# Hybrid decoder layer on eight cores: order of tiles, norm and branch results changed, and four tiles of x transposed by DMA

## The reference

```python
ya = pool_mixer(xa, pool_w, pool_scale) * silu(ga)
yb = u * (tril(w_s) @ layernorm(v) + b_s) * silu(gb)     # in chunks of 128 rows, 8 heads
yc = attention(q, k_mem, v_mem) * silu(gc)               # 4 heads over 256 memory rows
y = concat(rmsnorm(ya), rmsnorm(yb), rmsnorm(yc))
out = x + rmsnorm(y @ W_out) * norm_post
```

## Time and profile before

| what | value |
| --- | --- |
| median of three runs | 1258.14 us |
| the profiled execution | 1258.87 us |
| its span on the slowest core (core 3) | 1257.2 us |
| spans of all cores | 1251.3 to 1257.2 us |
| TensorE matmuls busy | 1220.3 us (97%) |
| VectorE, ScalarE, GpSimd busy | 488.0, 475.9, 216.0 us |

### The profile page before, as it was taken

How to read it: one execution, slowest core, us unless ns; L and a number is a source line. 1 busy time by engine, 2 the same in 40 slices (tenths; PEclk the granted TensorE clock), 3 DMA queues, 4 the chain that set the end, 5 groups by cost and what they waited for, 6 DMA issues and landing times.

```text
span 1257.2 us, 17843 instructions; the slowest of 8 cores (1251.3 to 1257.2 us)
## 1 busy us (share of the span) xinstructions
PE 1220.3 (97%) x6224; PEld 582.0 (46%) x6224; DVE 488.0 (39%) x782; ACT 475.9 (38%) x892; POOL 216.0 (17%) x205
## 2 busy tenths in 40 slices
PE   6889999999999999999999999999989999999997
PEld 3345544444444455555554444444434444444443
DVE  4167624332232233444443233333222454343434
ACT  4377733422222232222225555555632232223222
POOL 1000001221211011111121111111222222222222
PEclk9999999999999999999999999999999999999999
DMA  9945322554234452645435541441975492533231
GB/s 210 245 152 173 69 81 68 105 90 83 50 67 81 83 93 45 107 88 91 97 63 98 86 82 34 81 88 34 178 212 138 129 307 75 178 133 118 93 109 68
DMA packets 50938, 137.83 MB, mean 110 GB/s; under 512 B 22785, under 2 KB 35201, under 8 KB 37137
## 3 DMA queue, kind: packets, MB, share of 16 engines
q0 software_dynamic: 7632, 50.86, 24.3%
q1 hardware_dynamic: 43218, 85.83, 21.3%
HBM read 153.39 MB, written 29.36 MB: 145 GB/s over the span
## 4 chain that ended last, share of the span: by engine, by line
PE 90%; DMA 3%; DVE 2%; ACT 2%; issue 1%; SPq 0%; DVEq 0%; POOLq 0%; POOL 0%; ACTq 0%
PE ps L279 89%; DMA mem_pages<-x 2%; DMA mem_pages<-y_scr 2%; PE ps L282 1%; ACT mem_pages L391 1%; DVE mem_pages L395 1%; DVE mem_pages L1155 0%; ACT mem_pages L1030 0%; SPq L291 0%; ACT L1030 0%; DVE stat L1025 0%; DVE mem_pages L1127 0%; DVE mem_pages L1035 0%; DVE mem_pages L545 0%; ACT stat L256 0%
## 5 line engine op out<-in xcount | busy, mean ns | idle before, releaser
L279 PE MATMUL ps<-mem_pages 128*128 128x512 bf16 (+2 forms) x5760 | 1195.7, 369 | 7.9 <-DMA mem_pages<-y_scr 4.0
L279 PEld LDWEIGHTS ps<-mem_pages 128*128 128x128 bf16 x5760 | 555.7, 98 | 630.5 <-issue 22.8
L713 POOL TENSOR_TENSOR mem_pages<-mem_pages 128x512 f32<-128x512 f32 x72 | 91.1, 1266 | 599.9 <-ACT mem_pages L706 597.3
L700 ACT ACTIVATE mem_pages<-mem_pages,small_c 128x512 bf16<-128x512 f32 x96 | 68.8, 716 | 275.4 <-DVE mem_pages L772 148.1
L1127 DVE SCALAR_TENSOR_TENSOR mem_pages<-ps,stat,mem_pages 128x512 f32<-128x512 f32 x128 | 96.0, 750 | 166.8 <-PE ps L279 144.4
L1135 POOL TENSOR_TENSOR mem_pages<-mem_pages 128x512 f32<-128x512 f32 x64 | 81.1, 1267 | 257.3 <-ACT jk L1132 257.3
L1132 ACT ACTIVATE jk<-mem_pages 128x512 bf16<-128x512 f32 x64 | 40.3, 629 | 224.0 <-DVE mem_pages L1127 224.0
L903 DVE TENSOR_TENSOR mem_pages<-mem_pages 128x526 f32<-128x526 f32 (+3 forms) x80 | 56.1, 701 | 100.8 <-ACT mem_pages L897 95.8
L762 DVE TENSOR_TENSOR mem_pages<-ps,mem_pages 128x512 f32<-128x512 f32 x32 | 22.1, 691 | 141.3 <-PE ps L279 141.3
L732 ACT ACTIVATE mem_pages<-ps 128x512 f32<-128x512 f32 x96 | 54.5, 590 | 22.8 <-PE ps L279 19.4
L748 DVE CAST mem_pages<-ps 128x512 bf16<-128x512 f32 (+1 forms) x24 | 14.4, 601 | 124.6 <-PE ps L279 121.4
(11 more groups left out here) (66 smaller groups left out, 422.9 us busy)
## 6 DMA issues: line engine op xcount, KB each, us to landing
mem_pages<-w_pages POOLq DMA_DIRECT2D x44, 1024.0 KB, 12.9
mem_pages<-x SPq DMA_DIRECT2D x32, 1024.0 KB, 7.8
out<-mem_pages SPq DMA_DIRECT2D x15, 1024.0 KB, 4.7
y_scr<-mem_pages SPq DMA_DIRECT2D x96, 128.0 KB, 1.9
mem_pages<-y_scr SPq DMA_DIRECT2D x12, 1024.0 KB, 14.6
mem_pages<-w_pages POOLq DMA_DIRECT2D x8, 512.0 KB, 19.7
mem_pages<-mem SPq DMA_DIRECT2D x2, 1024.0 KB, 6.2
mem_pages<-mem_norm SPq DMA_DIRECT2D x1, 1024.0 KB
```

The costliest lines, as they stand in the source:

```text
L279: return lambda e: e.matmul(out, lhsT=lhsT, rhs=rhs, start=start, stop=stop)
L700: P.op("act", lambda e: e.activation(out=yv, in_=tmp, func=AF.Copy, scale=gbr[:, c:c + 1]), reads=[tmp_b[i], gbr_b], writes=[ring_b[r]])
L713: P.op("pool", lambda e: e.tensor_tensor(out=accl_v if last else acc, in0=acc, in1=dst, op=ALU.add), reads=[dst_b, acc_b[tb]], writes=[acc ...
```

## The change

It has five parts. In the front, the loads of tiles 4 and 5 of x wait for earlier weight tokens, the norm of tile 4 stands ahead of the LayerNorm halves, and the matmuls of tile 3 are spread between those of tiles 0 to 2. In the loop, tile 4's (1, 0) group comes ahead of tile 5's transposes, and a tile of x is loaded right behind the norm that frees its buffer. Tiles 9, 11, 13 and 15 are normed at the end of the turn three tiles earlier and transposed by one DMA each. In C, norm_post and y's first pages are loaded ahead of the third set of W_out pages. And the last tile's last 512 columns are worked in two halves of 256.

```diff
@@ -247,6 +247,7 @@
     ST_SSX, ST_RSX, ST_VS, ST_VQ, ST_VM, ST_VR, ST_VT = 0, 20, 40, 56, 72, 88, 104
     ST_RBR, ST_MX, ST_NB, ST_RI, ST_RS, ST_SO, ST_FO, ST_FR = 120, 168, 176, 184, 192, 256, 320, 336
     ST_LH0, ST_LH1 = 352, 360
+    ST_SL = 368
     ST_EPS = 383
 
     def sc(i):
@@ -546,7 +547,7 @@
                                               scalar2=sc(ST_VR + tt), op0=ALU.add, op1=ALU.mult),
              reads=[bank[b], bank[b + 1], s1], writes=[vn_b[tt]])
 
-    W2, W3, W4 = wbuf(("v", 0, 1)), wbuf(("v", 1, 0)), wbuf(("v", 1, 1))
+    W1, W3, W4 = wbuf(("v", 0, 0)), wbuf(("v", 1, 0)), wbuf(("v", 1, 1))
     x_a(0)
     x_a(1)
     x_a(2)
@@ -554,8 +555,8 @@
     x_pe(1, halves=(0,))
     x_a(3)
     x_pe(2, halves=(0,))
-    x_load(4, [W2[0].wtok])
-    x_load(5, [W4[0].wtok])
+    x_load(4, [W1[0].wtok])
+    x_load(5, [W3[1].wtok])
     x_load(6, [W4[1].wtok])
     x_load(7)
     x_pe(0, halves=(1,))
@@ -574,9 +575,9 @@
     for part in range(2):
         for tt in range(4):
             v_mm(tt, 0, 1, part)
-            if part == 1:
-                v_ln_half(tt, 0)
     x_a(4)
+    for tt in range(2):
+        v_ln_half(tt, 0)
     drop(*VN, dyn=False)
     take(*VN)
     vn_b += [nbuf("vn%d" % tt, VN[tt // 4]) for tt in range(NTT)]
@@ -584,19 +585,19 @@
         for tt in range(3):
             v_mm(tt, 1, 0, part)
     x_pe(4, (7, 7), (0,))
+    for tt in range(2, 4):
+        v_ln_half(tt, 0)
     v_mm(0, 1, 1, 0)
     v_mm(1, 1, 1, 0)
     x_pe(4, (7, 7), (1,))
     v_mm(2, 1, 1, 0)
-    v_mm(3, 1, 0, 0)
-    v_mm(3, 1, 0, 1)
     for tt in range(3):
+        v_mm(3, 1, tt // 2, tt % 2)
         v_mm(tt, 1, 1, 1)
         v_ln_half(tt, 1)
         v_ln_end(tt)
         if tt == 1:
             x_a(5)
-    v_mm(3, 1, 1, 0)
     v_mm(3, 1, 1, 1)
     v_ln_half(3, 1)
     v_ln_end(3)
@@ -630,20 +631,29 @@
                 out=tsg[:, h, :], in0=psb(b, q * 128, (q + 1) * 128), scalar=lnb[:, h:h + 1], in1=tsg[:, h, :],
                 op0=ALU.mult, op1=ALU.add), reads=[bank[b], tsg_b, small_b], writes=[tsg_b])
 
+    DT = (9, 11, 13, 15)
+    x_load(8)
+    x_load(9)
     for tt in range(4, NTT):
         v_mm(tt, 0, 0)
         v_mm(tt, 0, 1)
-        if tt + 1 < NTT:
+        if tt == 4:
+            v_mm(tt, 1, 0)
+        if tt + 1 < NTT and tt + 1 not in DT:
             x_pe(tt + 1)
-        if tt + 2 <= NTT:
+        if tt + 2 <= NTT and tt + 2 not in DT:
             x_a(tt + 2)
+            x_load(tt + 6)
         if tt + 2 == NTT:
             x_dma(NTT)
-        v_mm(tt, 1, 0)
+        if tt > 4:
+            v_mm(tt, 1, 0)
         v_mm(tt, 1, 1)
         v_ln(tt)
-        if tt + 4 <= NTT:
-            x_load(tt + 4)
+        if tt + 3 in DT:
+            x_a(tt + 3)
+            x_load(tt + 7)
+            x_dma(tt + 3)
         if tt + 4 > NTT:
             drop(xt_p[tt % NX])
             if tt == NTT - 1:
@@ -1099,7 +1109,7 @@
 
     def take_orow(tt):
         p = dyn()
-        orow[tt] = (p, [nbuf("or%d_%d" % (tt, db), p) for db in range(4)], nbuf("orr%d" % tt, p))
+        orow[tt] = (p, [nbuf("or%d_%d" % (tt, db), p) for db in range(5)], nbuf("orr%d" % tt, p))
 
     def load_xres(tt):
         p = dyn()
@@ -1107,55 +1117,56 @@
         dma_sp(page_f(p), x_d[tt * 128:(tt + 1) * 128, :], writes=[b], sem="d_ps%d" % p)
         xres[tt] = (p, b)
 
-    def wo_unit(tt, db):
+    def wo_unit(tt, db, lo=0, n=512, so=None):
         tb = tt // 4
+        so = ST_SO + tt * 4 + db if so is None else so
         p, obs, _ = orow[tt]
-        ov = page_f(p)[:, db * 512:(db + 1) * 512]
+        ob = obs[db + (1 if lo else 0)]
+        c0 = db * 512 + lo
+        ov = page_f(p)[:, c0:c0 + n]
         bks = []
         for br in range(3):
             b = balloc()
             yv = page_bf(ypage[(tb, br)][0]).rearrange("p (c t) -> p c t", c=8)
             Wo = w8(("wo", db, br))
-            fns = [mm(psb(b), yv[:, q, (tt % 4) * 128:(tt % 4 + 1) * 128], Wo[:, q, :], q == 0, q == 7)
+            fns = [mm(psb(b, 0, n), yv[:, q, (tt % 4) * 128:(tt % 4 + 1) * 128], Wo[:, q, lo:lo + n], q == 0, q == 7)
                    for q in range(8)]
             P.group("pe", fns, reads=[ypage[(tb, br)][1], wbuf(("wo", db, br))], writes=[bank[b]])
             bks.append(b)
         rc = ST_RBR + tt
-        P.op("act", lambda e: e.activation(out=ov, in_=psb(bks[0]), func=AF.Identity, scale=sc(rc)),
-             reads=[bank[bks[0]], rbr_b[tb]], writes=[obs[db]])
+        P.op("act", lambda e: e.activation(out=ov, in_=psb(bks[0], 0, n), func=AF.Identity, scale=sc(rc)),
+             reads=[bank[bks[0]], rbr_b[tb]], writes=[ob])
         for br in (1, 2):
             P.op("dve", lambda e, br=br: e.scalar_tensor_tensor(
-                out=ov, in0=psb(bks[br]), scalar=sc(rc + br * 16), in1=ov, op0=ALU.mult, op1=ALU.add),
-                reads=[bank[bks[br]], rbr_b[tb], obs[db]], writes=[obs[db]])
+                out=ov, in0=psb(bks[br], 0, n), scalar=sc(rc + br * 16), in1=ov, op0=ALU.mult, op1=ALU.add),
+                reads=[bank[bks[br]], rbr_b[tb], ob], writes=[ob])
         bfree(*bks)
-        so = ST_SO + tt * 4 + db
-        P.op("act", lambda e: e.activation(out=jk_v, in_=ov, func=AF.Square, scale=D ** -0.5, accum_out=sc(so)),
-             reads=[obs[db]], writes=[jk_b, so_b[tt]])
-        gv = page_f(gp["p"])[:, db * 512:(db + 1) * 512]
+        P.op("act", lambda e: e.activation(out=jk_v[:, 0:n], in_=ov, func=AF.Square, scale=D ** -0.5,
+                                           accum_out=sc(so)),
+             reads=[ob], writes=[jk_b, so_b[tt]])
+        gv = page_f(gp["p"])[:, c0:c0 + n]
         P.op("pool", lambda e: e.tensor_tensor(out=ov, in0=ov, in1=gv, op=ALU.mult),
-             reads=[obs[db], gp["b"]], writes=[obs[db]])
+             reads=[ob, gp["b"]], writes=[ob])
 
     so_b = [Buf("so%d" % t) for t in range(NTT)]
 
     def wo_final(tt, last=False):
         p, obs, _ = orow[tt]
         stf = Buf("stf")
-        c0 = ST_SO + tt * 4
-        P.op("dve", lambda e: e.reduce_sum(out=sc(ST_FO + tt), in_=stat[:, c0:c0 + 4], axis=AX.X),
+        c0, cn = (ST_SL, 5) if last else (ST_SO + tt * 4, 4)
+        P.op("dve", lambda e: e.reduce_sum(out=sc(ST_FO + tt), in_=stat[:, c0:c0 + cn], axis=AX.X),
              reads=[so_b[tt]], writes=[stf])
         rstd_of(sc(ST_FR + tt), sc(ST_FO + tt), stf)
         xp, xb = xres[tt]
-        n = 4 if last else 1
-        w = 2048 // n
         rows = out_d[tt * 128:(tt + 1) * 128, :]
-        for q in range(n):
-            o = page_f(p)[:, q * w:(q + 1) * w]
-            xv = page_f(xp)[:, q * w:(q + 1) * w]
-            ob = obs if n == 1 else [obs[q]]
+        pieces = [(q, 1, obs[q:q + 1] if q < 3 else obs[3:]) for q in range(4)] if last else [(0, 4, obs)]
+        for q, n, ob in pieces:
+            o = page_f(p)[:, q * 512:(q + n) * 512]
+            xv = page_f(xp)[:, q * 512:(q + n) * 512]
             P.op("dve", lambda e, o=o, xv=xv: e.scalar_tensor_tensor(out=o, in0=o, scalar=sc(ST_FR + tt), in1=xv,
                                                                      op0=ALU.mult, op1=ALU.add),
                  reads=[stf, xb] + ob, writes=ob)
-            dma_sp(rows[:, q * w:(q + 1) * w], o, reads=ob, sem="d_o%d_%d" % (tt % 4, q))
+            dma_sp(rows[:, q * 512:(q + n) * 512], o, reads=ob, sem="d_o%d_%d" % (tt % 4, q))
         drop(p, xp)
         orow.pop(tt)
         xres.pop(tt)
@@ -1165,8 +1176,8 @@
         gp["b"] = nbuf("gpost", gp["p"])
         dma_sp(page_f(gp["p"]), norm_post_d.partition_broadcast(128), writes=[gp["b"]], sem="d_g")
 
-    out_q = [(3, 0, lambda: wo_load(0)), (3, 0, lambda: wo_load(1)), (3, 0, lambda: wo_load(2)),
-             (3, 13, lambda: y_load(0)), (2, 0, gp_load)]
+    out_q = [(3, 0, lambda: wo_load(0)), (3, 0, lambda: wo_load(1)), (1, 10, gp_load), (3, 12, lambda: y_load(0)),
+             (3, 13, lambda: wo_load(2))]
 
     for n in range(len(blocks)):
         hh, tb = blocks[n]
@@ -1226,9 +1237,13 @@
         if tt % 4 == 0 and tt // 4 + 1 < 4:
             y_load(tt // 4 + 1)
         take_orow(tt)
-        for db in range(4):
-            wo_unit(tt, db)
-        wo_final(tt, last=tt == NTT - 1)
+        last = tt == NTT - 1
+        for db in range(3 if last else 4):
+            wo_unit(tt, db, so=ST_SL + db if last else None)
+        if last:
+            wo_unit(tt, 3, 0, 256, ST_SL + 3)
+            wo_unit(tt, 3, 256, 256, ST_SL + 4)
+        wo_final(tt, last)
         if tt + 2 < NTT:
             load_xres(tt + 2)
         if tt % 4 == 3:
```

## The result

The changed kernel takes **1274.03 us** (median of four runs, 1270.98 to 1279.48) against 1258.62 us for the kernel before in the same series: ratio 1.0126, interval 1.0084 to 1.0169. It is slower by some 16 us; the forecast was 12 faster. In some executions of these kernels the cores of one die run at a lower granted clock and take longer; they are left out of every time and ratio here. The profiled execution took 1271.12 us. Its slowest core is core 5 with a span of 1268.4 us, and the cores lie further apart than before: 1250.6 to 1268.4. Lines above 250 have moved on by one: L280 is every matmul, L283 every transpose on TensorE, L292 SP's plain DMAs, L295 the weight loads, L419 the DMA transpose.

The account below looks back on a forecast made before the run. The prediction took TensorE's own work, 90% of the chain of waits, as the bound. Its terms, -7.1 + 0.9 - 5.7 - 0.4 = -12.3 us, gave 1246.6 against the profiled run, 1246 against the median; range 1239.5 to 1252.

Parts of the forecast that it names:

- tile 13's stall: V stage: TensorE waits for tile 13's DMA transpose, issued with a weight page; 0 to 4.4 us, taken 2.0.
- Tile 9: V stage: its DMA transpose stands behind one x load in SP's queue; stall 0 to 2.7 us, taken 1.0.
- the third rival: V stage: weight pages issued just behind or with the DMA transposes starve them; total 1271; chance 0.07.
- Tile 11: V stage: DMA transpose behind an x load, with a weight page in flight; stall 0 to 4 us, taken 1.5.
- Tile 15: V stage: DMA transpose issued after the next page is nearly down; stall 0 to 1.5 us, taken 0.
- The saving: V stage: 4 x 16 transposes leave TensorE's path, 3.56 us; with stalls of 4.5 a net cost of 0.9.
- The front: Start of kernel: gap near 45 us and slow matmuls go, tile 6's transposes near 71; -7.1 us, bounds 4.5 and 9.7.
- the second rival: Front bound by transfer: TensorE waits for sixth to eighth weight halves, stall about 3.5 us, total 1249.5; chance 0.15.
- Output loads: Before the output: 4.0 us of y_scr waits and 1.7 of slow matmuls go; -5.7 us, bounds 2.3 and 5.7.
- Last tile: End of kernel: halved final columns shorten the steps after the last matmul; -0.4 us, bounds -0.3 and 0.7 gained.

## Why the prediction was wrong

**The step that failed is tile 13's stall** in the sum: the prediction let it run from 0 (the transpose gets ahead) to 4.4 (it waits for the page's lone landing of 9.1), and took 2.0. Measured: 19.4 to 21.7 us on the odd cores, 8.0 to 8.2 on cores 0, 4 and 6. The upper bound was no bound. It took the page's landing from a row where the page flew alone and let the transpose at worst wait for it. But each slows the other: run in turn they take 13.2 us, side by side 14 to 16 on the even cores and 27 to 30 on the odd ones. I had a row that pointed there: a transpose beside three pages took 19.9. I read it as waiting for the backlog, which made the price a matter of how many pages stand ahead, and one page harmless. A bound for "beside a page" should have come from that row (19.9 - 5.6, a stall of 14), however far it seemed; even that is short of the odd cores' 21.7. The sentence that the slowest core falls by about as much as the others failed with it, since the cores' stalls differ by more than 10 us.

**Tile 9** was priced 1.0 (0 to 2.7). Core 5 shows 1.43, three even cores 8.1 to 8.3. Missed in the sum was the page issued just as tile 9 is due; I had it only in the third rival. With the transpose ahead of the x load it lands 0.9 to 1.9 us before that page is issued, and no core waits. **Tile 11**: 1.5 priced, 1.40 measured on core 5. **Tile 15**: 0, and it landed in 4.3.

Some of the working was off by itself, too little to matter: 9.1 against 5.6 gives a stall of 3.5 and not 4.4; no row gives tile 9's upper 2.7 (5.5 of the load and 5.3 of its own against 5.8 would be 5.0); tile 7's matmuls start at 90.6 by the addition shown, not 90.4; and 9.62 is 1.8 over 7.8, not 1.7.

**Slow matmuls behind a stall** (2.5 us on core 5) were in the rival and not in the sum. They came behind the 21.17 us there, and on core 2 already behind 2.26 (5.30 for 16 matmuls), while core 3 has none behind 2.19 (3.61). **The saving** of 3.56 is real in count, but even with clean landings only 0.8 us of it by the times, or 1.8 by the spans, is left, since TensorE waits 1.1 for VectorE at tile 10 and up to 1.0 at tile 11. I had costed the removed copies and the moved norm on VectorE at nothing beside other work.

**The front** was priced -7.1 (4.5 to 9.7). Alone it measures -8.7 (5.3 to 12.1). The gap at 45 us and the slow matmuls behind it went as told; tile 6's transposes stand at 72.1 and 73.1 on the cores shown (before 78.30, forecast 71.2), which is 5 to 6 of the 8.7, and the weight stalls of the second rival exist (0.3 and 1.4) but are less than half of its 3.5. **Output loads**: -5.7 forecast, -6.8 measured (4.4 to 9.2), through the mechanism named. **Last tile**: -0.4, within its bounds and below what can be measured. Without the tiles by DMA the forecast's terms come to -13.2; measured -14.5.

**The third rival came true**, at a chance of 0.07. Its total of 1271 is near 1274; its places were partly right (tile 13 longest, tile 9 on even cores). Its price for tile 13 (11 us, two pages) was still half of what the odd cores show, and its reason was again a backlog; that the totals lie so close is luck. Held against it was that each backlog was of one page only: that argument fell with the run in which only the second page was held.

On the Trainium skill: its rule that an engine takes turns between queues packet by packet (DMA: Bandwidth & Descriptors, "Queues, rings and completion order") pointed to the side on which the time fell, and the landings of 14 to 15 for both are compatible with it. That the page itself goes from 9 to 28 us does not follow from it as I used it. The sentence that transposes are as fast as other DMAs (Advanced Engine Details and Errata, "X-Bar Transpose (TRN2)") is not settled here for a lone one: 0.5 MB in 4.3 us keeps pace with a weight page (1 MB in 8.7) but not with a load of x (1 MB in 5.5). It does not hold for one in flight together with a page.

**Open.** Why odd and even cores differ by a factor of two at tile 13 wasn't settled; in the kernel before, transposes beside three pages took 18.5 to 21.3 on all cores alike. An obvious rival, that neighbouring cores meet, was not tried; against the plain form of it stands that with the second page held odd cores issue tile 13's transpose at 123 to 124 or, behind a stall at tile 9, at 132.8, and it lands after 25.5 there and after 24.2 and 24.3 here, which is the same within 1.3 us. Nor was it tried whether the cast of the weight load, its queue or its size is what collides with the transpose.

## What to carry to other kernels

Before you move work from an engine to a DMA, list what else is in flight when it must land: two transfers that are short alone can hold each other up for much longer than both in turn, so price "beside" only from a row where both fly, take its whole landing, and leave room above it (that row would have given 14 us here, and 21 came). A wait that puts the bulk load behind the small urgent transfer costs nothing where the load has slack, and here it turned 21 us into none. And compare with doing without: the cured version is not measurably faster than TensorE's own transposes, which need none of this care.

## What the runs showed of the hardware

A DMA transpose of 128x2048 bf16 within SBUF lands in 4.2 to 5.3 us alone, in 7 to 11 behind an x load of 1 MB, and at tile 13 in 14 to 32 beside a weight load of 1 MB that casts float32 to bfloat16. That load takes 8.3 to 9.1 alone and 14 to 32 beside it. In four microseconds of this the DMA engines count as more than busy (2.01) while 72 GB/s pass, so a busy share says nothing of progress there.

At tile 9 cores that run one program, with the same 5.8 us between transpose and page, wait 1.1 to 2.2 us or 8.1 to 8.3. The time of issue does not sort them: core 5's transpose, issued at 93.19, landed after 7.4, core 0's, issued at 93.10, after 14.1. Which cores are hit changes from execution to execution. An average over cores would hide this; the slowest core, which is the metric, showed first one cause, and when it was cured, the other.
